# Selecting the rows of eight expert steps on TensorE from the residual in SBUF instead of gathering them from memory, in a one-core decoder layer with a mixture of experts

## The reference

```
x  += merged @ w_out
h2  = rmsnorm(x, g_ffn)                       # 512 x 1024
idx, wts = route(h2, ...)                     # 8 of 64 experts per token
moe = sum over the 8 experts e of a token: wts * (silu(h2 @ w_gate[e]) * (h2 @ w_up[e])) @ w_down[e]
moe += swiglu(h2, w_sh_gate, w_sh_up, w_sh_down)          # shared expert
x  += moe
x  += sigmoid(rmsnorm(x) @ w_ple_gate) * rmsnorm(p @ w_ple_proj)
```

## Time and profile before

| | us |
|---|---|
| median of 3 runs | 987.73 (987.58 to 988.1) |
| the profiled execution, its own time | 983.44 |
| its span on the core | 981.6 |
| PE busy | 937.8 (96%) |
| DVE, ACT, POOL busy | 364.7, 163.8, 229.2 |

### The profile page before, as it was taken

How to read it: one execution, slowest core, us unless ns; L and a number is a source line. 1 busy time by engine, 2 the same in 40 slices (tenths; PEclk the granted TensorE clock), 3 DMA queues, 4 the chain that set the end, 5 groups by cost and what they waited for, 6 DMA issues and landing times.

```text
span 981.6 us, 15774 instructions
## 1 busy us (share of the span) xinstructions
PE 937.8 (96%) x6407; PEld 490.9 (50%) x6407; DVE 364.7 (37%) x787; ACT 163.8 (17%) x306; POOL 229.2 (23%) x344
## 2 busy tenths in 40 slices
PE   9999999999999999999999999999879899898888
PEld 7688888888556533333333333354323233332345
DVE  3765774236436733333333111011101111111887
ACT  2001233210011211111111111111101112111121
POOL 4216913262000212222222222212121211201120
PEclk9999999999999999999999999999989999999999
DMA  9970006422473799999999999999999999999982
GB/s 334 384 246 1 1 1 214 129 86 86 144 297 110 246 385 384 396 420 410 399 423 405 412 414 405 411 422 421 414 421 421 421 419 418 419 402 362 347 313 86
DMA packets 86009, 305.08 MB, mean 311 GB/s; under 512 B 9389, under 2 KB 38097, under 8 KB 61744
## 3 DMA queue, kind: packets, MB, share of 16 engines
q1 hardware_dynamic: 72240, 267.38, 69.4%
q0 software_dynamic: 11920, 33.46, 8.7%
q10 hardware_dynamic: 1776, 3.21, 0.9%
HBM read 279.26 MB, written 33.55 MB: 319 GB/s over the span
## 4 chain that ended last, share of the span: by engine, by line
PE 73%; DMA 21%; SPq 2%; DVE 2%; issue 1%; ACT 0%; ACTq 0%; DVEq 0%
PE ps L2300 22%; DMA ring<-in_w_exp_up 18%; PE ps L1903 13%; PE ps L2329 8%; PE ps L2053 6%; PE ps L2032 5%; PE ps L2447 4%; PE ps L1812 2%; PE ps L1845 2%; DMA ring<-in_w_exp_down 2%; PE ps L2124 1%; PE ps L1855 1%; DMA ring<-accumulator 1%; SPq L555 1%; PE ps L2309 1%; SPq L541 1%
## 5 line engine op out<-in xcount | busy, mean ns | idle before, releaser
L2300 PE MATMUL ps<-ring,gates 128*32 128x512 f32 x2560 | 287.1, 600 | 27.9 <-DMA ring<-in_w_exp_up 27.1
L2300 PEld LDWEIGHTS ps<-ring,gates 128*32 128x32 f32 x2560 | 88.3, 111 | 218.7 <-issue 217.8
L2329 PE MATMUL ps<-ring,poolbuf 128*32 128x512 f32 x1280 | 147.3, 601 | 3.0 <-DMA ring<-in_w_exp_down 2.1
L1615 DVE COPY poolbuf<-ps 128x256 f32<-128x256 f32 x40 | 17.0, 425 | 355.8 <-PE ps L2309 355.8
L809 POOL TENSOR_TENSOR tickets<-cst 128x1 f32<-128x1 f32 x77 | 14.5, 188 | 398.2 <-ACT actT L1012 392.8
L2329 PEld LDWEIGHTS ps<-ring,poolbuf 128*32 128x32 f32 x1280 | 38.3, 110 | 84.6 <-issue 83.0
L1012 ACT ACTIVATE actT<-ps,qT 128x1024 f32<-128x1024 f32 x40 | 44.5, 1113 | 143.9 <-PE ps L2329 143.9
L1004 ACT ACTIVATE poolbuf<-ps 128x256 f32<-128x256 f32 x40 | 15.4, 384 | 279.6 <-PE ps L2300 279.6
L1903 PE MATMUL ps<-xrow,ring 128*128 128x256 f32 x256 | 57.9, 381 | 0.1
L2053 PE MATMUL ps<-ring,gates 128*128 128x512 f32 x128 | 56.4, 594 | 0.0
L1903 PEld LDWEIGHTS ps<-xrow,ring 128*128 128x128 f32 x256 | 48.3, 190 | 8.4 <-issue 1.7
(11 more groups left out here) (306 smaller groups left out, 1086.3 us busy)
## 6 DMA issues: line engine op xcount, KB each, us to landing
ring<-in_w_exp_down SPq DMA_DIRECT2D x64, 1024.0 KB, 17.3
ring<-in_w_exp_gate SPq DMA_DIRECT2D x62, 1024.0 KB, 13.5
ring<-in_w_exp_up SPq DMA_DIRECT2D x62, 1024.0 KB, 16.5
ring<-accumulator SPq DMA_DIRECT2D x10, 1024.0 KB, 13.5
ring<-in_w_gate SPq DMA_DIRECT2D x8, 1024.0 KB, 11.8
accumulator<-ring SPq DMA_DIRECT2D x2, 4096.0 KB, 22.6
ring<-in_w_in SPq DMA_DIRECT2D x5, 1024.0 KB, 10.1
ring<-accumulator SPq DMA_DIRECT2D x10, 512.0 KB, 9.5
```

What stands on the lines that cost most here:

```text
L2300: last = mm(bank(2 + k)[part, :], hgT[k][:, q, part], pair_view(EXPERT_SLOT[js[c]])[:, q], start=(q == 0), stop=(q == KD - 1))
L2329: last = mm(bank(6 + half)[part, :], eactT[r % 2][:, q, part], w[:, q, half * 512:(half + 1) * 512], start=(q == 0), stop=(q == 1))
```

## The change

Steps 28 to 35 (CHOSEN) are no longer gathered. For such a step r, DVE builds a 0/1 matrix in the free buffer `hg` (a place equals a token's rank in that expert's list), times the token's reciprocal norm (`choose`, issued at step r - 2). TensorE multiplies the residual `xrow` by it (`chosen_T`, in the place of `rows_T`): for each of 8 slices of 128 columns and each of 4 tiles of tokens one product of 128x128 by 128x128. That gives the transposed rows at once, and DVE multiplies both banks by the gain on their way to `hgT`; ACT's copy of bank 1 falls away. Because the residual must not change before its last selection (step 35's, made in step 34), the shared additions move from steps 30 to 33 (one in a slot) to steps 34 and 35 (two in a slot), and the p products from steps 34 to 37 to steps 36 to 39. POOL skips the eight gathers, and loads one more small tile (`gffn_col`) early in the kernel.

```diff
-JOB_STEP = [SMALL_AT + n // 2 for n in range(8)] + [SMALL_AT + 6 + n // 2 for n in range(4 * NT)]
+JOB_AT = [(SMALL_AT + n // 2, n % 2) for n in range(8)] + \
+    [(SMALL_AT + 10 + n // 4, n % 4 // 2) for n in range(2 * NT)] + \
+    [(SMALL_AT + 12 + n // 2, n % 2) for n in range(2 * NT)]
+CHOSEN = range(SMALL_AT + 4, SMALL_AT + 12)
...
+        chosen = [h[:, 0:NT * P].rearrange("p (i n) -> p i n", i=NT) for h in hg]
...
+            small_load(gffn_col[:, :], t["g_ffn"].rearrange("o (p k) -> (o p) k", k=KD))
...
-                if not last:
+                fetched = gathers(range(min(r + BUF + 1, STEPS)))
+                if not last and r + BUF not in CHOSEN:
                     pool.wait_ge(hgT_ps, 2 * r + 2)
...
                     gather(j)
...
-                if r + 1 < STEPS:
+                if r + 1 < STEPS and r + 1 not in CHOSEN:
                     rows_hi(r + 1, (r + 1) % 2)
...
+            def choose(r):
+                g, s = STEP_OF[r]
+                dve.wait_ge(hgT_ps, 2 * (r - BUF) + 2)
+                at = chosen[r % BUF]
+                e, cap = g * GROUP + pair_of(g, s), cap_of(g)
+                link(nc.vector.tensor_tensor(
+                    at.rearrange("p i (e r) -> p i e r", r=cap),
...
+                    rank3[:, :, e:e + P // cap].unsqueeze(3).broadcast_to([P, NT, P // cap, cap]), ALU.is_equal))
+                nc.vector.tensor_tensor(at, at, st[:, 1, 0:NT].unsqueeze(2).broadcast_to([P, NT, P]), ALU.mult
+                                        ).then_inc(rows_ready, 1)
+            def chosen_T(r, k):
...
+                for half, done in enumerate((hgT_lo_ready, hgT_hi_ready)):
+                    dve.wait_ge(hgT_ps, 2 * r + half + 1)
+                    nc.vector.tensor_tensor(
+                        hgT[k][:, 4 * half:4 * half + 4, :], bank(half).rearrange("p (k n) -> p k n", k=4),
+                        gffn_col[:, 4 * half:4 * half + 4].unsqueeze(2).broadcast_to([P, 4, P]), ALU.mult
+                    ).then_inc(done, 1)
...
-                if r + 1 < STEPS:
+                if r + 1 in CHOSEN:
+                    chosen_T(r + 1, (r + 1) % 2)
+                elif r + 1 < STEPS:
                     rows_T(r + 1, (r + 1) % 2)
+                if r + 2 in CHOSEN:
+                    choose(r + 2)
...
-                    pe.wait_ge(small_loaded, 16 * 10)
+                    pe.wait_ge(small_loaded, 16 * 11)
...
+            def chosen_T(r):
+                pe.wait_ge(rows_ready, NT + CHOSEN.index(r) + 1)
+                pe.wait_ge(hgT_lo_ready, r)
+                pe.wait_ge(hgT_hi_ready, r)
+                v = xrow.rearrange("p i (q k) -> p i k q", k=KD)
+                for half in range(2):
+                    for k in range(4):
+                        for i in range(NT):
+                            last = mm(bank(half)[:, k * P:(k + 1) * P], v[:, i, 4 * half + k, :],
+                                      chosen[r % BUF][:, i, :], start=(i == 0), stop=(i == NT - 1))
+                    last.then_inc(hgT_ps, 1)
...
-                if r + 1 < STEPS:
+                if r + 1 in CHOSEN:
+                    chosen_T(r + 1)
+                elif r + 1 < STEPS:
                     rows_T(r + 1)
```

More of the change, by code:

```diff
@@ L77, in jobs_of, with gathers @@
 def jobs_of(step, slot):
-    return [n for n, at in enumerate(JOB_STEP) if at == step and n % 2 == slot]
+    return [n for n, at in enumerate(JOB_AT) if at == (step, slot)]
+def gathers(steps):
+    return sum(1 for r in steps if r not in CHOSEN)
 def cap_of(g):
@@ L209, in build @@
         gcol = sb("gcol", [P, KD])
+        gffn_col = sb("gffn_col", [P, KD])
         sink_in = sb("sink_in", [P, NH])
@@ L836, in move @@
                     if not first:
-                        pool.wait_ge(ticket_done[0], r)
-                    pool.wait_ge(staged, 2 * r + BUF + 1)
+                        pool.wait_ge(ticket_done[0], fetched - BUF - 1)
+                    pool.wait_ge(staged, r + fetched)
                     ticket(0, ticket_done[0])
@@ L845, in move @@
                     pool.wait_ge(ticket_done[1], r)
-                pool.wait_ge(staged, STEPS + r + 1 if last else 2 * r + BUF + 2)
+                pool.wait_ge(staged, fetched + r + 1)
                 pool.wait_ge(y_ready, r + 1)
@@ L864, in o_move @@
                 pool.wait_ge(o_over, n + 1)
-                pool.wait_ge(ticket_done[0], STEPS - BUF + n)
+                pool.wait_ge(ticket_done[0], gathers(range(BUF, STEPS)) + n)
                 pool.wait_ge(o_list_ready, n + 1)
@@ L1606, in rows_T @@
                                       ).then_inc(hgT_lo_ready, 1)
+            def choose(r):
[5 more added lines that the diff above has]
+                    at.rearrange("p i (e r) -> p i e r", r=cap),
+                    cst[:, C_IOTA + CAP - cap + 1:C_IOTA + CAP + 1].unsqueeze(1).unsqueeze(1).broadcast_to(
+                        [P, NT, P // cap, cap]),
+                    rank3[:, :, e:e + P // cap].unsqueeze(3).broadcast_to([P, NT, P // cap, cap]), ALU.is_equal))
+                nc.vector.tensor_tensor(at, at, st[:, 1, 0:NT].unsqueeze(2).broadcast_to([P, NT, P]), ALU.mult
+                                        ).then_inc(rows_ready, 1)
+            def chosen_T(r, k):
+                if r == CHOSEN[0]:
+                    dve.wait_ge(small_loaded, 16 * 11)
+                for half, done in enumerate((hgT_lo_ready, hgT_hi_ready)):
[4 more added lines that the diff above has]
+                    ).then_inc(done, 1)
             def act_rows(r, k):
@@ L2268, in rows_T @@
                 j = r % BUF
-                pe.wait_ge(gathered[j], 16 * (r // BUF + 1))
+                pe.wait_ge(gathered[j], 16 * gathers(range(j, r + 1, BUF)))
                 if r:
```

## The result

The changed kernel takes 1072.02 us (median of 6 runs, 1070.41 to 1075.44) against 987.65 us before (6 runs): a ratio of 1.0863 with a 95% interval of 1.0845 to 1.0882, 84 us slower. The prediction had the sign and a fifth of the size: +17, with a range that ended at 1012. The profiled execution took 1070.55 us, its span is 1067.9 us.

The account below looks back on a forecast made before the run. DMA bounds steps 28 to 39; with 7.0 us selections PE becomes the bound from step 27, and DMA's saving buys nothing. Selecting steps, packed jobs and the end make +17 us on 987.73: 1004.7, range 997 to 1012.

Parts of the forecast that it names:

- What bounds the kernel: Steps 28 to 39 bound by DMA, with about 25 us of spare PE time; after the change PE bounds from step 27.
- DMA's part: Eight gathers less save 8.7 us of DMA time, 1.09 us each; a gain only if DMA alone set the end.
- TensorE's part: A selection is 64 instructions at 0.11 us, 7.0 us in all, 6.1 more than what it replaces; bounds 6.9 and 12.2.
- rival (c): In the selections, weight loads don't overlap because xrow is read with a stride of 8: 12.2 us each, 1046; chance 0.03.
- main case: PE-bound selecting steps with 7.0 us a selection: 17 us slower, 1004.7 us; chance 0.87 together with gathers that save DMA nothing.
- The moved jobs: Shared additions and p products packed two in a slot: step 34 takes 26.7 us, step 35 20.6, steps 36 to 38 15.2 each.
- The end: After down(38), a p product and its followers take 4.0 us before down(39), 19.7 later; DVE's next addition 17.2 later.
- The sum: PE's steps from up(27) on added up: down(38) ends at 915.9 us instead of 898.9, 17.0 later.
- The range: Whole time of 997 to 1012 us, counting 0.1 us more or less for each selection among the doubts.
- Rival (a): Selections of one instruction a product take 3.5 us, DMA bounds to step 34, end about 3 us earlier, 984.7; chance 0.06.

Follow-up runs that it names:

- e5: Changed kernel with selection over one of four token tiles, neighbouring columns as weights, jobs at their old steps: 979.06 us, against 985.7 for the kernel before.
- e9: Whole change with the selection turned round: rank matrix as weight, 512 neighbouring residual columns moved, rows copied and then transposed: 1015.31 us.
- e1: Changed kernel with 128 neighbouring residual columns as weights of a selecting product instead of every eighth one: 1009.96 us.
- e12: Changed kernel with weights still strided by eight, but 512 columns moved by each selecting product (32 instructions a selection): 1060.53 us.
- e4: Changed kernel with the selecting product's operands exchanged: rank matrix as weight, residual moved with its stride of eight: 1074.84 us.
- e7: Kernel before with only the shared additions and p products moved to steps 34 to 39, gathers kept: 992.81 us, 1.0085 times before.
- e10: Against the kernel before: three selections in steps 28 to 30, rank matrix as weight, jobs one step later: 982.05 us against 986.64, ratio 0.9956.

## Why the prediction was wrong

- **What bounds the kernel, and DMA's part**: right. Steps 28 to 39 were bound by DMA, and e5 shows the eight gathers worth 6.6 us by its one time and 7.9 by the start of its `down(38)`, against 8.7. (PE's need in the ten steps adds up to 148, not 149; nothing hangs on it.) DMA fell below full at once, to a share of 0.71 in step 28, and not after step 33.
- **TensorE's part: the step that failed.** "I take 0.11: a selection is 7.0 us ...; the ends are 6.9 and 12.2." It measured 15.22, above the upper end. The reason given in rival (c), "the transposes at 0.11 read strided rows too", carried a property of transposes over to products. Transposes read this stride for nothing (0.88 for eight, also in e9); a float32 product with 128 moving columns takes 0.238 us an instruction with it and 0.112 without (e1). For neighbouring columns the term was right: 7.15 against 7.0. The upper end was wrong too: it was the length of a contiguous weight load, 0.19 us, and a strided one is recorded with 335 ns, one starting every 238.
- **Rival (c)**, put at 0.03 and +58, named the cause, the stride of 8 elements, but not what it does. Weight loads that don't overlap weren't the mechanism: the strided load hides behind 512 moving columns (e12), and a strided moving operand pays as much (e4). The price was larger too: 8 x (15.22 - 7.0) = 65.8 us beyond the main case. The stride should have been given far more: no row before showed a strided product.
- **The moved jobs**: 35.3 and 21.1 us for steps 34 and 35, where 26.7 + 8.2 and 20.6 were worked out; steps 36 to 38 at 15.5 for 15.2. Right within 0.5 each.
- **The end**: `down(39)` starts 3.95 us after `down(38)` ends, forecast 4.0. The span from `down(39)` to the end is 79.6 for 81.4 before, 1.8 shorter, 2.5 forecast; that the sizes are near is luck. The prediction let what follows move with DVE's addition. That starts 8.68 us behind `down(39)` before and 7.10 after, in both cases still behind the sum that waits for the rows read back. But the next transposes on PE stand behind PE's own 16 products of picked rows, and start 10.71 us behind `down(39)` in both traces (the kernel before, then after):

```profile
903.86 7.06 PE ps L2372 x16
910.93 0.23 PE ps L2431 x2
```
```profile
991.94 7.06 PE ps L2427 x16
999.01 0.23 PE ps L2486 x2
```

  The two run alike to 22.5 us behind `down(39)`. The 1.8 us come later, 0.8 of them where DVE waited 0.75 us for rows read back in the kernel before and no longer waits.
- **The sum, made again with the measured selection**: 17.2 + 65.8 = 83.0; `up(27)` 0.6 later, the jobs' steps 1.9, the end 0.7 and the rest 0.1 make the 86.3 by which the span grew. With e1's selection of 7.15 and its `up(27)` 4.6 later, the same terms give 17.2 + 1.2 + 4.6 + 1.9 + 0.7 = 25.6, and e1's span (1007.3) grew by 25.7: beside the selection the sum was off by some 3 us.
- **The range** failed with the term: its bounds took 0.1 us of doubt for each selection, from a row that was no measurement of it.
- **Rival (a)**, a cheap selection with the jobs packed, was given a gain of 3 us. e7 shows the packing alone costs 7 to 8 with the gathers in place, about what the gathers give; a selection that cheap with the jobs packed wasn't run.

## What to carry to other kernels

Price a matmul by a row of its own kind: a transpose and a product, or the same product with contiguous operands, don't stand for each other when an operand has a stride. A stride of 32 bytes is best put on a transpose, or on the weights of a product with 512 moving columns, where it was free here, and not on a product with 128. A strided moving operand of 512 columns wasn't tried. Work that is moved off a queue that is full onto an engine with spare time has to be placed step by step: three selections gave nothing with one of them in a step that was already busy, and 0.4% where each step had time.

## What was not expected of the hardware

- A float32 product of 128 by 128 columns takes 0.112 us an instruction with neighbouring columns, 0.118 with a stride of 8 bytes, 0.233 with 16 and 0.238 with 32, and the moving operand pays like the weights (0.233 with 32).
- A transpose with weights strided by 32 bytes takes 0.11 us, as long as one with neighbouring columns (four in 0.44, the shared expert's transposes in step 27 of e10). Why it is spared is open; nothing here tried it.

```profile
695.40 0.44 PE ps L2284 x4
```

- The products at the start of the kernel, 0.236 us an instruction, have neighbouring columns. They aren't slow for their shape (e1: 0.112), and the transposes right behind them are slow by the same factor, 1.91 us for eight against 0.88 later. So that stretch runs at about half the later rate, though its granted clock reads 1.00 in the trace, and its nearness to the strided 0.238 says nothing of a stride. Why it is slow is open.
